# Grid attention: the products with the keys' low parts over half the rows, two scores as row tiles

## The reference

```
GRID_W = 64; C_HEADS = 16; HEAD_DIM = 64; NA_ROWS = 8; NA_COLS = 16

def one(r):                                   # one grid row of 64 tokens
    rs = clip(r - kr // 2, 0, rows - kr)
    kblk = dynamic_slice_in_dim(kg, rs, kr)    # 8 grid rows of keys
    s = einsum('bqhd,bikhd->bhqik', qblk, kblk) * scale + bias
    s = where(colmask, s, -inf)                # 16 columns around the query
    p = softmax(s)
    return einsum('bhqik,bikhd->bqhd', p, vblk)
```

## Time and profile before

| | |
|---|---|
| median of 3 runs | 2372.94 us (2372.34 to 2373.17) |
| span of the profiled execution | 2368.2 us |
| median less span | 4.7 us |
| TensorE busy in the span | 2275.0 us, 96% |
| VectorE, ScalarE, GpSimd busy | 1610.3, 1312.2, 687.2 us |

### The profile page before, as it was taken

One profiled execution on the slowest core, in us unless ns is written; L12 is line 12 of the kernel. 1 busy time (PEld: TensorE's weight loads), 2 busy tenths in 40 slices (PEclk: granted clock), 3 DMA queues, 4 the chain that ended last, 5 costly groups with the idle time before them and its releaser, 6 DMA issues. The chain is left out here.

```text
span 2368.2 us, 35378 instructions
## 1 busy us (share of the span) xinstructions
PE 2275.0 (96%) x11782; PEld 1932.6 (82%) x11782; DVE 1610.3 (68%) x3297; ACT 1312.2 (55%) x3022; POOL 687.2 (29%) x843
## 2 busy tenths in 40 slices
PE   7999999999999999999999999998998999999999
PEld 6888788888887878888888888787777888887887
DVE  7443677677886433346665566669889788889787
ACT  6444566666775434446656566555555645455542
POOL 3455232311245542222222221655553300000000
PEclk9999999999999999999999999999999999999999
DMA  7322101111233332322332233532352633345734
GB/s 226 118 72 64 39 26 34 32 34 46 63 122 109 98 130 67 94 67 88 91 94 74 90 89 94 189 89 77 92 171 85 196 103 107 119 139 174 230 111 140
DMA packets 331203, 241.68 MB, mean 102 GB/s; under 512 B 66320, under 2 KB 284688, under 8 KB 330512
## 3 DMA queue, kind: packets, MB, share of 16 engines
q1 hardware_dynamic: 331024, 239.42, 33.2%
HBM read 195.59 MB, written 43.78 MB: 101 GB/s over the span
## 5 line engine op out<-in xcount | busy, mean ns | idle before, releaser
L2850 POOL TENSOR_TENSOR WS<-WR,WS 128x256 fp32r<-128x256 f32 x635 | 495.0, 799 | 1019.2 <-ACT WS L2184 1018.1
L1934 PE MATMUL PS<-HT,WS 128*128 128x512 f32 x1492 | 603.9, 405 | 18.7 <-POOL WS L2850 5.5
L1936 PE MATMUL PS<-HT,WS 128*128 128x512 f32 x1492 | 585.1, 392 | 0.0
L1935 PE MATMUL PS<-HT,WS 128*128 128x512 f32 x1492 | 583.8, 391 | 0.0
L1934 PEld LDWEIGHTS PS<-HT,WS 128*128 128x128 f32 x1492 | 282.1, 189 | 78.6 <-issue 14.5
L1936 PEld LDWEIGHTS PS<-HT,WS 128*128 128x128 f32 x1492 | 281.6, 189 | 61.7
L1935 PEld LDWEIGHTS PS<-HT,WS 128*128 128x128 f32 x1492 | 282.7, 189 | 52.1
L2184 ACT ACTIVATE PT<-PS 128x512 fp32r<-128x512 f32 x352 | 186.0, 529 | 203.4 <-PE PS L2047 203.0
L2184 ACT ACTIVATE WS<-WR 128x256 fp32r<-128x256 f32 x658 | 245.6, 410 | 91.7 <-PE PS L1936 60.3
L2432 DVE TENSOR_TENSOR PT<-PS,PT 128x512 fp32r<-128x512 f32 x352 | 211.3, 609 | 93.8 <-ACT PT L2184 91.5
L2080 PE MATMUL PS<-PT,QKV 128*128 128x256 f32 (+1 forms) x1248 | 207.3, 287 | 3.2 <-DVE YB L2611 2.3
(11 more groups left out here) (286 smaller groups left out, 4587.9 us busy)
## 6 DMA issues: line engine op xcount, KB each, us to landing
WR<-in_w_in_odd SPq DMA_DIRECT2D x106, 256.0 KB, 2.9
EO<-in_grid SPq DMA_DIRECT2D x48, 384.0 KB, 3.1
WR<-in_ffn_in SPq DMA_DIRECT2D x60, 256.0 KB, 3.0
WR<-in_w_in_even SPq DMA_DIRECT2D x100, 128.0 KB, 2.5
WR<-in_w_out_odd SPq DMA_DIRECT2D x48, 256.0 KB, 2.8
yd<-PY SPq DMA_DIRECT2D x44, 256.0 KB, 3.4
EO<-in_ffn_in SPq DMA_DIRECT2D x35, 256.0 KB, 3.1
WR<-in_w_in_even SPq DMA_DIRECT2D x34, 256.0 KB, 2.9
```

The costliest lines, as they stand in the source:

```text
L1934: e.matmul(out, wh, rh, start=start, stop=False)
L1935: e.matmul(out, wh, rl, start=False, stop=False)
L1936: return e.matmul(out, wl, rh, start=False, stop=stop)
L2850: e.tensor_tensor(ws(i, 1, n), RAW[raw_slot(u)][:, o:o + n], f32(ws(i, 0, n)), ALU.subtract).then_inc(s_wlop.sem, 1)
```

## The change

In grid chunks the steps of a score are put together anew. The step of `x = 0` issues only its first product (full height, 128 rows). The step of `x = 1` issues its own first product and then the second products of both scores, each over only the 64 rows on which the queries' high part stands. For `x = 0` these are `HALF[h]`, for `x = 1` `HALF[1 - h]`, so that the two matmuls use different row halves, and they write to different banks. To have the high part of the second half's queries on the other 64 partitions, their layout is exchanged: ScalarE writes the rounded part to both halves (four writes in place of two), and VectorE puts the low part where the first of the two stood. Low times low falls away. The diff:

```diff
             if h.kind in ("k", "kg"):
                 a, v = a // 2, v // 2
+            if h.kind == "qg" and h.n == 1:
+                a = 4
...
                     for sig, value in ready[c.wants[0]] + ready[c.wants[1]]:
                         w.wait_ge(sig, value)
+                    if c.grid:
+                        bank = s.banks[0]
+                        w.wait_ge(*until[bank])
+                        col = (0, 8, 24, 32)[s.pp]
+                        kh, kl = [], []
+                        for x in (0, 1):
+                            for part, to in ((0, kh), (1, kl)):
+                                to.append(k_at(c.kv_slot, h, part).rearrange("p (r c) -> p r c", c=64)[:, 4 * x:4 * x + 12, col:col + 32])
+                        q = [q_at(c.q_slot, h)[:, 512 * x + 128 * s.pp:512 * x + 128 * s.pp + 128] for x in (0, 1)]
+                        out = [PS[:, B_S + x, 0:384].rearrange("p (r c) -> p r c", c=32) for x in (0, 1)]
+                        e.matmul(out[s.x], q[s.x], kh[s.x], start=True, stop=False)
+                        until[bank] = (s_mx, s.mx)
+                        if s.x == 1:
+                            for x in (0, 1):
+                                rows = HALF[h ^ x]
+                                e.matmul(out[x], q[x][rows], kl[x][rows], start=False, stop=True).then_inc(s_score.sem, 1)
+                        continue
...
-                            if c.grid:
-                                q = q_at(c.q_slot, h)[:, 512 * s.x + 128 * s.pp:512 * s.x + 128 * s.pp + 128]
-                                col = (0, 8, 24, 32)[s.pp]
-                                kh, kl = (k_at(c.kv_slot, h, part).rearrange("p (r c) -> p r c", c=64)[:, 4 * s.x:4 * s.x + 12, col:col + 32]
-                                          for part in (0, 1))
-                                out = out.rearrange("p (r c) -> p r c", c=32)
-                            else:
-                                q = q_at(c.q_slot, h)[:, qt]
-                                kh, kl = (k_at(c.kv_slot, h, part, a, a + s.cut) for part in (0, 1))
+                            q = q_at(c.q_slot, h)[:, qt]
+                            kh, kl = (k_at(c.kv_slot, h, part, a, a + s.cut) for part in (0, 1))
...
                     elif h.kind == "qg":
                         for x in (0, 1):
-                            act(by_tiles(q_at(slot, x, a, b))[HALF[x]], of_rows(ps)[HALF[x]], scale=1.0).then_inc(s_ea.sem, 1)
+                            for y in (0, 1)[:h.n + 1]:
+                                act(by_tiles(q_at(slot, x, a, b))[HALF[x ^ y]], of_rows(ps)[HALF[x]], scale=1.0).then_inc(s_ea.sem, 1)
...
-            def put_grid_q(ps, slot, a, b, ea):
+            def put_grid_q(ps, slot, a, b, ea, n):
+
                 for x in (0, 1):
                     dst = by_tiles(q_at(slot, x, a, b))
-                    w.wait_ge(s_ea, ea + x + 1)
-                    take(dst[HALF[1 - x]], of_rows(ps)[HALF[x]], dst[HALF[x]]).then_inc(s_ed.sem, 1)
+                    w.wait_ge(s_ea, ea + (n + 1) * (x + 1))
+                    take(dst[HALF[1 - x ^ n]], of_rows(ps)[HALF[x]], dst[HALF[x]]).then_inc(s_ed.sem, 1)
```

More of the change, by code:

```diff
@@ L2494, in vector_program @@
                     elif h.kind == "qg":
-                        put_grid_q(ps, slot, a, b, h.ea)
+                        put_grid_q(ps, slot, a, b, h.ea, h.n)
                     else:
```

## The result

The changed kernel takes 2385.96 us (median of 4 runs, 2384.9 to 2388.55) against 2373.06 us for the kernel before beside it: 12.9 us more. The ratio is 1.0061, with a 95% interval of 1.0046 to 1.0077. It is slower, clear of the 0.2% that a measurement can tell. The time lies inside the stated range (2361 to 2390), and not where I put the likeliest case (2375.2); it lies in the rival on the other side, the switch that waits.

The account below looks back on a forecast made before the run. TensorE alone was taken to bound the grid-score stage. Two 0.08 us switches against a 0.07 to 0.18 us gain made +0.035 us over 64 units, +2.2 us: about 2375.2 us, likeliest 2371.6 to 2378.7, 8-in-10 range 2361 to 2390.

Parts of the forecast that it names:

- the likeliest case: Whole kernel: pair gain against two switches of 0.08 us, net +2.2 us, 2371.6 to 2378.7; chance 0.33.
- What bounds the stage: Grid-score stage: TensorE alone sets the time, busy 64.9 of 65 us; each microsecond there counts, except last-chunk waits.
- (a): Second products in a unit: overlap of the half-height pair gains 0.07 to 0.18 us, or 0 without overlap.
- (b): Switching between full and half height, twice a unit: 0.08 us each taken, bounds 0 to 0.27.
- The bound of 0.27: Upper bound for one switch: the matmul before completes (0.16 us), then the load runs uncovered (0.11).
- the decision point: A switch costing more than half the pair's gain, 0.09 us, decides for the waiting switch.
- (c): Order and waits of a unit's four products: cost 0, or 0.2 us a unit if the cover were gone.
- (d): Exchanged query layout: 9.5 us more ScalarE work, VectorE up to 1.2 us later; cost 0, or 9.6 uncovered.
- (e): DMA: nothing is issued, removed or moved on any queue.
- waiting switch: Rival: each switch waits 0.16 us for the matmul before; +9 to +16 us, 2381.9 to 2388.9; chance 0.29.
- The marks: Signs in a changed unit: its four score matmuls taking under 0.73 or over 0.89 us would prove the forecast wrong.
- The second mark: Sign for the waiting switch: a unit's four score matmuls together take 0.94 us or more.

Follow-up runs that it names:

- e12: Changed kernel without the grid scores' second products and with the old layout of the queries, in more rounds: 2355.42 us, ratio 0.9928.
- e4: Changed kernel without the grid scores' second products, exchanged layout of the queries kept: 2362.51 us, ratio 0.9959.
- e6: Changed kernel with the half-height pair issued first, then the two full-height first products: 2385.83 us, ratio 1.0053.
- e3: Changed kernel with each half-height second product right behind its own first product, four switches a unit and no pair: 2418.59 us, ratio 1.0192.
- e8: Changed kernel with the half-height pair over 128 of its 384 columns: 2378.81 us, ratio 1.0031.
- e10: Changed kernel with second products over all 128 rows and the old layout of the queries, so only the order is new: 2373.15 us, ratio 0.9999.
- e9: Changed kernel with second products over all 128 rows, new order and exchanged layout kept, in more rounds: 2372.69 us, ratio 0.9998.
- e2: Changed kernel with both half-height second products on the same 64 rows and the old layout of the queries: 2393.34 us, ratio 1.0089.

## Why the prediction was right or wrong

**What bounds the stage.** Right. TensorE is busy 65.00 of 65 us after, and what a unit lost came out in the time, but for 0.2 us a chunk. For shorter units the other engines are nearer than I had it: I let the last chunk swallow an eighth of a gain, and of 23 us 5 did not come out in e12 and 12 not in e4. The median was not 4.7 us above the span for what lies around it, as I wrote: each listed time of the kernel before is 1.8 us above its own span, and the other 2.9 say that the profiled execution was a fast one. The forecast took this as a constant and is not touched.

**(a) The gain.** I left it open between 0.07 and 0.18 us a unit and took the middle. It is 0.18: the pair starts together, loads too. The lower end came from supposing that half-height loads behave as full-height ones do, each starting with the matmul before it. The two loads of a pair don't: they start together. By the Trainium skill, TensorE: Matmul & The Clock Gate, Part 3, The mechanism, matmuls on different row groups start some 4 ns apart; the trace agrees, with 0.45 us for two against 0.442 for one.

**(b) The switch: the step that failed.** I took 0.08 us, from the change of transposes to matmuls, as the nearest row. It measured 0.19 to 0.20, more than twice, in both directions. The nearest row was not a smaller case of the same thing; it was no price at all, as the sum beside e6 shows, but the place where a row is drawn. The same holds for L1934 after transposes. So the forecast's term had nothing behind it, and it should have been a range from 0 to 0.27. My own bounds held what happens. A switch load starts 0.27 us after the matmul before it has begun, 0.09 later than that one's interval of 0.18, and then its 0.11 us are uncovered, since the matmul needs it: 0.20. The bound of 0.27 had both terms, with 0.16 for the first, the modelled end of a result; 0.16 alone was the other case, and it set the upper end of my range. The true value has a shorter wait (0.09) and the load in the open (0.11). So the range held by some luck: the case that it took in had the wait too long and the load left out, and the two errors nearly cancel. I had named the decision point, 0.09 us a switch; it was passed.
The Trainium skill, TensorEngine Tiling (Array Packing), Key Properties, says that a change of tiling mode drains TensorE. The runs agree as far as they go: no load starts until some 0.09 us after the interval of the matmul before, and the price hangs on the number of changes (e3), not on the columns (e8).

**(c), (d), (e).** (c) right: 2373.15 against 2373.19 in e10. One reading in it was off: VectorE's second score read ends at 1209.51, some 4.5 us ahead of the next scores at 1213.97, not 8; that is still ample. (d) off by 1 us: I put it at nothing, looking at PT, the score reads and the weight splits, and the cover fails once, in the seventh chunk, where the transposes of the reciprocals wait for VectorE's subtraction (1.1 us in e9 against e10, 0.9 in the changed kernel's wait). No such wait was on my list of signs. (e) right.

**The rivals and the chances.** The waiting switch had 0.29 and +9 to +16 us; it came with +12.9. The forecast with 0.33 was 10.8 us too low, nearly all of it in (b), less what (a) gave back: (0.19 - 0.08) x 2 - (0.18 - 0.125) = +0.165 us a unit, 64 x 0.165 = 10.6 us. That this meets 10.8 so closely has luck in it too, as 0.2 us a chunk go and 1 us comes from (d). The marks: the four matmuls took 0.90 us. That is just past the 0.89 at which I said I would be wrong, and short of the 0.94 that I gave the waiting switch. The second mark was off, as the last 0.10 us of the second switch stand behind the four, in front of the transposes of PT (0.58 us from L2092 to L2059, 0.48 before).

## What to carry to other kernels

Half-height matmuls on the two row halves do run beside each other, but price the passage into and out of half height first: here 0.19 us each, a little more than a whole 384-column matmul. One pair between full-height work loses; count how many pairs stand together before laying data out for it. Where the trace prices only a different kind of change, keep it as one end and not as the middle: add what the new change could make uncovered (here one load, 0.11 us) on each side. And before a longer distance between two rows is called a price, add up the distances over the whole group: here the first product's distance was 0.08 us long only because the last transpose's was 0.08 us short. To compare two kernels more sharply than their medians do, take the same stretch of work from both traces; here it agrees to 0.01 us in 260, and showed a wait of 1.1 us that the medians hid.

## What the runs showed of the hardware

Passing between 128-row and 64-row matmuls costs 0.19 to 0.20 us in each direction at a granted clock of 1.00, with no semaphore in it: about 0.09 us of waiting past the interval of the matmul before, and a load of 0.11 us that nothing covers. The columns of the matmul before (384 or 128, e8) don't change it. The loads of the two row halves overlap as well (0.19 us for two, 0.30 for four). The first matmul behind a switch has a modelled duration of 0.44 us in place of 0.34, whether it has 64 rows or 128 (e3), because its row includes the uncovered load; it doesn't hold TensorE longer than that. Two matmuls on the same 64 rows keep the interval of 0.18 us (e2).
